# A two-block transformer kernel on one core: a reordered latent stage, and matmul operands at other byte offsets

## The chip, the core and the metric

The kernel runs on one core of a Trainium2 chip. A core has a matrix engine (TensorE, PE in the profile), three engines for elementwise work (VectorE or DVE, ScalarE or ACT, GpSimd or POOL), and SyncE (SP), which issues most of the loads. Each engine runs its own program in order; they meet through semaphores. Matmul operands lie in SBUF, 128 partitions wide; results go to eight PSUM banks. The metric is the device time of one execution in microseconds.

## The reference, cut to what matters

Two blocks over a sequence of 512 tokens and a width of 1,024, all in float32:

```python
# first block: layer 0 is a short convolution mixer, layer 1 latent attention
h = h + short_conv_mixer(rms_norm(h, ...), a_w_in, a_conv, a_w_out)
h = h + conv_ffn(rms_norm(h, ...), up 0, conv, down 0)
ckv = rms_norm(h, kv_in_norm) @ w_dkv                    # 1024 -> 256 + 64
c_kv, k_rope = ckv[..., :256], apply_rope(ckv[..., 256:], cos, sin)
kv = rms_norm(c_kv, kv_norm) @ w_ukv                     # 256 -> 8 heads x (128 + 128)
q = rms_norm(rms_norm(h, ...) @ w_dq, q_norm) @ w_uq     # 1024 -> 512 -> 8 x (128 + 64)
h = h + causal_attention(q, k, v) @ w_o
h = h + conv_ffn(rms_norm(h, ...), up 1, conv, down 1)
# second block: modulation from c, three mixers side by side
#   (spatial gating, stick breaking, dilated windows), then
x = x + (1 + gate1) * (mixers @ w_out)
x = x + (1 + gate2) * conv_ffn(..., up 2, conv, down 2); return rms_norm(x)
```

## The kernel before, in words

Activations lie transposed: features on the partitions, in chunks of 128, and the 512 tokens along the row. A product of one weight tile (8 blocks of 128 x 128) with an activation goes into one PSUM bank of 512 columns. To keep float32 accuracy both sides are split into a high half (fp32r) and a low half, and `dot` (lines 1466 to 1468) issues three matmuls for each block: high x high, high weights x low activation, low weights x high activation. `wide` runs `dot` over the eight chunks of an activation.

The high and low halves of activations have their own buffers: XH and XL (inputs of most products, all up stages among them), MH and ML (mixer output, stage A_OUT), HH and HL (hidden layer, the three down stages), QXH and QXL (input of DQ), CLH and CLL (k and v latent, input of UKV), OH and OL (attention output, stage WO). All of these, and the weight buffers WH and WL, begin at a multiple of LINE = 2,048 bytes. The buffers of one stage share memory with those of others by stacks that are closed again, and what is allocated after a pair in its stack begins behind it.

A weight tile comes by a DMA of SyncE into one of four raw slots. ScalarE copies it to WH (line 554, called by `hi`; `ahead(t)` waits until TensorE has done tile t and then converts tile t + 2), and GpSimd subtracts, WL = raw - WH (line 505). In the up stages VectorE makes WL instead (line 968). WH and WL have two slots each.

The stage that the change reorders lies between the first feed-forward network and the attention, about 550 to 625 us. TensorE's order: three products DKV (two chunks of the k and v latent, and the 64 k_rope features, doubled), four products DQ, then UKV in four tiles, then UQ. Between them it forms column sums of squares: N_KV inside the first DKV product, N_LK (norm of the k and v latent) after the second DQ product (line 1506), N_LQ (norm of the q latent) after the second product of UKV's first tile, by eight one-column matmuls (`token_squares`, line 1511).

VectorE's order: reciprocal rb; the eight low halves QXL (line 898); for each of two DKV products the eviction times rb into CL (line 1107) and the add of its square (line 887); the whole `rope` of the third DKV product (line 1081 eviction times rb into RA, 1086 four products of 32 partitions with the sine table, 1090 the product with the cosine table, 1097 the sum into KR); `inverse(N_LK)` (line 891, and a memset of acc, 893); CL times rbl (line 1113), CLL (898); then for each of four DQ products the eviction into QL (1118) and the add of its square; then the evictions of UKV.

ScalarE's order: squares of CL; `ahead(T0["DQ"])`; the root of N_LK (line 583); `ahead(T0["DQ"] + 1)`; CLH (line 710); then for k = 0 to 3 the square of QL's chunk k, with `ahead(T0["DQ"] + k)` in front of it for k = 2 and 3. `ahead(T0["DQ"] + 2)` is what converts the first tile of UKV.

Of the kernel before, what the change touches and what calls it, by code (L numbers as in the profile page):

```python
# [18 lines left out]
F32R = mybir.dt.float32r  # L19
# [15 lines left out]
KQ, KKV = Q_LORA // P, KV_LORA // P
# [20 lines left out]
LINE = 4 * S  # L56
# [61 lines left out]
def build(nc, w_tiles, ada_tiles, c_in, x_in, vec_in, const_in, rope_in, mask1_in, mask2_in, gsgu_in, wsp_in, pos_in, out):  # L118
    T0, M0, DONE_T, DONE_M = schedule()
# [5 lines left out]
    with ctx:  # L125
        def sb(name, shape, dt=F32, stack=ctx, align=32):
            return stack.enter_context(nc.sbuf_tensor(name, shape, dt, align_bytes=align))

        def sem(name):
            return ctx.enter_context(nc.semaphore(name))  # L130

# [18 lines left out]
        cos_t, sin_t = trig[:, 0, :], trig[:, 1, :]  # L150
        rb = sb("rb", [P, S])
        rbl = sb("rbl", [P, S])
        acc = sb("acc", [P, S])
# [3 lines left out]
        RA, RB = RAB[:, 0, :], RAB[:, 1, :]  # L157


        st = ExitStack()  # L160
        CV = sb("CV", [P, KD, S], F32, st)
        MH = sb("MH", [P, KD, S], F32R, st, align=LINE)
        ML = sb("ML", [P, KD, S], F32R, st, align=LINE)
        st.close()
        st = ExitStack()
        HH = sb("HH", [P, FF, S], F32R, st, align=LINE)
        HL = sb("HL", [P, FF, S], F32R, st, align=LINE)
        st2 = ExitStack()
        TG = sb("TG", [P, S + 16], F32, st2)
        TU = sb("TU", [P, S + 16], F32, st2)  # L170
# [6 lines left out]
        ADA_SLOT = (ada01[:, 0, :], ada01[:, 1, :], trig[:, :, :].rearrange("p a b -> p (a b)"))  # L177
        crow = RAB[:, :, :].rearrange("p a b -> p (a b)")
        st = ExitStack()
        QXH = sb("QXH", [P, KD, S], F32R, st, align=LINE)  # L180
        QXL = sb("QXL", [P, KD, S], F32R, st, align=LINE)
        st.close()
        st = ExitStack()
        KN = sb("KN", [P, HEADS, S], F32, st)
        VT = sb("VT", [P, HEADS, S], F32, st)
        KR = sb("KR", [P, S], F32, st)
# [6 lines left out]
        CLL = sb("CLL", [P, KKV, S], F32R, st2, align=LINE)  # L193
        QL = sb("QL", [P, KQ, S], F32, st2)
        st2.close()
        OH = sb("OH", [P, HEADS, S], F32R, st, align=LINE)
        OL = sb("OL", [P, HEADS, S], F32R, st, align=LINE)
        st.close()
        st = ExitStack()
        FT = sb("FT", [P, 12, S], F32, st)  # L200
# [37 lines left out]
        ps = [ctx.enter_context(nc.psum_tensor(f"ps{i}", [P, S], F32)) for i in range(8)]  # L238
# [4 lines left out]
        s_in = {n: sem(f"s_in_{n}") for n in ("x0", "x1", "x2", "x3", "c", "vec", "const", "rope", "gsgu", "wsp", "mask", "pos")}  # L243
# [5 lines left out]
        s_ev = sem("s_ev")  # L249
# [10 lines left out]
        s_ssum = sem("s_ssum")  # L260
        s_root = sem("s_root")
        s_rb = sem("s_rb")
# [21 lines left out]
        s_qk = sem("s_qk")  # L284
# [44 lines left out]
        def vcol(name, i):  # L329

            first = V[name][0]
            return vec[:, first + i:first + i + 1] if isinstance(i, int) else vec[:, bass.ds(i + first, 1)]
# [17 lines left out]
        N_A, N_F0, N_KV, N_LK, N_LQ, N_F1, N_FIN, N_F2, N_END = range(9)  # L350
# [3 lines left out]
        E_A, E_F0, E_KV, E_Q, E_F1, E_M2, E_F2 = range(7)  # L354

        XL0 = [KD * e for e in range(E_M2 + 1)] + [KD * E_M2 + KD // 2]
        RB_AT = {n: i for i, n in enumerate((N_A, N_F0, N_KV, N_LK, N_F1))}
# [184 lines left out]
        def _(act):  # L542
            ch = Chain(act, s_act)
# [136 lines left out]
            def a_b(i):  # L680
                for k in range(4):
                    ahead(T0["A_B"] + k, i, 4)
                    act.wait_ge(s_y, i * 4 + (k + 1))
                    apart()
                    nc.scalar.activation(at(MH, i * 4 + k), CU[:, :], ACT.Copy).then_inc(s_yh, 1)
            repeat(act, 2, a_b)
# [21 lines left out]
            for m in range(KKV):  # L708
                act.wait_ge(s_nb, NB_KV + m + 1)
                nc.scalar.activation(CLH[:, m, :], CL[:, m, :], ACT.Copy, scale=vcol("kv_norm", m)).then_inc(s_lh, 1)  # L710
            for k in range(KQ):
                if k > 1:
                    ahead(T0["DQ"] + k)
                act.wait_ge(s_ev, M0["DQ"] + k + 1)
                square(N_LQ, k, k, QL[:, k, :])
# [20 lines left out]
            for a in range(BLOCKS_A):  # L736
                L = (block_a(a)[1] + 1) * P
                if a >= 4:
# [7 lines left out]
                                     scale=stat[:, 3, a:a + 1]).then_inc(s_pn, 1)  # L746
# [127 lines left out]
        def _(dve):  # L874
            ch = Chain(dve, s_dve)
            v = nc.vector
# [6 lines left out]
            def add_square(n, m, k):  # L883
                dve.wait_ge(s_sq, m + (SQ0[n] + 1))
                if not (n == 0 and isinstance(m, int) and m == 0):
                    dve.wait_ge(s_acc, m + ACC0[n])
                v.tensor_tensor(acc[:, :], acc[:, :], SQ[:, k % 2, :], ALU.add).then_inc(s_acc, 1)  # L887

            def inverse(n, dst):
                dve.wait_ge(s_root, n + 1)  # L890
                v.reciprocal(dst[:, :], dst[:, :]).then_inc(s_rb, 1)
                dve.wait_ge(s_rb, RB_AT[n] + 1)
                ch.link(v.memset(acc[:, :], 0.0))
# [175 lines left out]

            ropes = [0]  # L1070

            def rope(M, dst, scale=1.0, by=None):


                if ropes[0]:
                    dve.wait_ge(s_qk, ropes[0])
                ropes[0] += 1
                product(M)
                x = ps[M % 4]
                if by is not None:  # L1080
                    v.tensor_tensor(RA[:, :], x[:, :], by[:, :], ALU.mult).then_inc(s_ev, 1)
                    dve.wait_ge(s_ev, M + 1)
                    x = RA
                for row in range(0, P, 32):
                    other = row ^ 32
                    ch.step(v.scalar_tensor_tensor(RB[row:row + 32, :], x[other:other + 32, :], scale,  # L1086
                                                   sin_t[other:other + 32, :], ALU.mult, ALU.mult))
                if by is not None:
                    ch.wait()
                ins = v.scalar_tensor_tensor(RA[:, :], x[:, :], scale, cos_t[:, :], ALU.mult, ALU.mult)  # L1090
                if by is None:
                    ins.then_inc(s_ev, 1)
                    dve.wait_ge(s_ev, M + 1)
                    ch.wait()
                else:
                    ch.link(ins)
                v.tensor_tensor(dst, RA[:, :], RB[:, :], ALU.add).then_inc(s_qk, 1)

            def take(aux, dst):
# [5 lines left out]
            for k in range(KKV):  # L1105
                product(M0["DKV"] + k)
                v.tensor_tensor(CL[:, k, :], ps[(M0["DKV"] + k) % 4][:, :], rb[:, :], ALU.mult).then_inc(s_ev, 1)
                add_square(N_LK, k, k)
            dve.wait_ge(s_in["rope"], 32)
            rope(M0["DKV"] + KKV, KR[:, :], by=rb)  # L1110
            inverse(N_LK, rbl)
            for m in range(KKV):
                v.tensor_tensor(CL[:, m, :], CL[:, m, :], rbl[:, :], ALU.mult).then_inc(s_nb, 1)
            for m in range(KKV):
                lo_half(CLH[:, m, :], CLL[:, m, :], CL[:, m, :], vcol("kv_norm", m), (s_lh, m + 1), s_ll)
            for k in range(KQ):
                product(M0["DQ"] + k)
                v.tensor_tensor(QL[:, k, :], ps[(M0["DQ"] + k) % 4][:, :], rb[:, :], ALU.mult).then_inc(s_ev, 1)
                add_square(N_LQ, k, k)

            for t in range(HEADS // 2):
                for j in range(4):
                    M = M0["UKV"] + 4 * t + j
# [20 lines left out]
            for h in range(HEADS):  # L1144
                M = M0["UQ"] + HEADS // 2 + h
# [303 lines left out]
        def _(pe):  # L1449
# [20 lines left out]
            def wide(t, M, i=0, per=0, before=None, src=(XH, XL), ready=True, within=None):  # L1470

                if ready:
                    tile_ready(t, i, per)
                bank_free(M, i, per)
                for k in range(KD):
                    if before:
                        before(k)
                    last = dot(ps[M % 4][:, :], t, k, src[0][:, k, :], src[1][:, k, :], k == 0, k == KD - 1)
                    if within is not None and k == 5:
                        sum_squares(within)  # L1480
                last.then_inc(s_pe, 1)
# [15 lines left out]
            def inputs(e):  # L1497

                if e < E_M2:
                    return lambda k: pe.wait_ge(s_xl, KD * e + k + 1)  # L1500
                return lambda k: pe.wait_ge(s_xlp, XLP0[e] + k // 2 + 1) if k % 2 else \
                    pe.wait_ge(s_xl, XL0[e] + k // 2 + 1)

            def sum_squares(n):
                pe.wait_ge(s_acc, ACC0[n + 1])
                mm(ps[4][:, :], cc("ones"), acc[:, :], start=True, stop=True).then_inc(s_ssum, 1)
# [37 lines left out]

            out_product("A_OUT", (MH, ML), lambda k: pe.wait_ge(s_yl, k + 1))

# [83 lines left out]
            for k in range(3):  # L1630
                wide(T0["DKV"] + k, M0["DKV"] + k, before=inputs(E_KV) if k == 0 else None,
                     within=N_KV if k == 0 else None)
            for k in range(KQ):
                wide(T0["DQ"] + k, M0["DQ"] + k, before=inputs(E_Q) if k == 0 else None, src=(QXH, QXL))
                if k == 1:
                    sum_squares(N_LK)
            for t in range(HEADS // 2):
                tile_ready(T0["UKV"] + t)
                for j in range(4):
                    M = M0["UKV"] + 4 * t + j  # L1640
# [16 lines left out]
            for t in range(6):  # L1657
                tile_ready(T0["UQ"] + t)
                for j in range(2):
                    M = M0["UQ"] + 2 * t + j  # L1660
# [12 lines left out]
            for a in range(BLOCKS_A + 4):  # L1673
                if a < BLOCKS_A and a % 2 == 0:
                    for c in (a, a + 1):
                        h, qb = block_a(c)
# [7 lines left out]
                    for c in (a, a + 1):  # L1684
                        h, qb = block_a(c)
# [13 lines left out]
                if 0 <= b:  # L1699
                    h, qb = block_a(b)  # L1700
# [304 lines left out]
```

## Time and profile before

| | |
|---|---|
| median of 3 runs | 1811.03 us (1807.66 to 1811.35) |
| profiled execution, its own time | 1807.92 us |
| its span in the profile | 1806.2 us |
| TensorE matmul busy | 97% of the span |
| VectorE busy | 64% |
| ScalarE busy | 38% |
| GpSimd busy | 22% |

Times in the trace count from the start of the span. A TensorE matmul's record is longer than the distance to the next one's start, because matmuls overlap; the pace of the engine is read from the distances of the starts. "Idle before" is the time in which the engine had nothing running ahead of an instruction, and behind the arrow stands what released it. The granted clock is 1.00 at 2.4 GHz and 0.50 at 1.2 GHz.

### The profile page before, as it was taken

The numbers are of one execution on the slowest core, as the hardware profiler recorded it, in microseconds if no ns is written. First come the engines' busy times: TensorE is split into PE (matmuls) and PEld (weight loads), VectorE is DVE, ScalarE is ACT, GpSimd is POOL, SyncE is SP. The second block draws the span as 40 slices with busy tenths as digits, with TensorE's granted clock in tenths as the row PEclk, the third lists the DMA queues.
The fourth block names the chain that finished last, engine by engine and source line by source line (L and its number), as shares of the span: only waits on it lengthen the run. The fifth ranks groups of instructions, "written<-read, shape, count | busy, mean of one in ns | idle before, by whom it ended". The sixth has DMA issues, their size and how long they took to land.

```text
span 1806.2 us, 22183 instructions
## 1 busy us (share of the span) xinstructions
PE 1749.3 (97%) x7818; PEld 1412.7 (78%) x7818; DVE 1150.2 (64%) x1498; ACT 694.5 (38%) x967; POOL 396.2 (22%) x170
## 2 busy tenths in 40 slices
PE   7999999999999899999999999999999899999997
PEld 6888788888887666778888888787558788888886
DVE  6566777776667765577777766574756577777222
ACT  4123444443223235444444322332563444444221
POOL 3444100001444330210000144444101300000343
PEclk9999999999999899999999999999999899999999
DMA  4332232224663220132322466322100232222331
GB/s 181 101 108 93 93 104 94 93 98 159 221 210 105 70 71 1 59 105 93 101 96 93 148 234 212 108 94 90 39 1 24 70 105 93 99 99 93 105 105 70
DMA packets 52187, 186.84 MB, mean 103 GB/s; under 512 B 5792, under 2 KB 6048, under 8 KB 52000
## 3 DMA queue, kind: packets, MB, share of 16 engines
q1 hardware_dynamic: 50832, 182.47, 29.8%
q10 hardware_dynamic: 1296, 3.58, 0.6%
q8 instruction: 37, 0.61, 0.1%
q14 instruction: 22, 0.18, 0.0%
HBM read 183.94 MB, written 2.10 MB: 103 GB/s over the span
## 4 chain that ended last, share of the span: by engine, by line
PE 87%; DVE 8%; ACT 2%; issue 1%; DMA 1%; POOL 0%; ACTq 0%; DVEq 0%; SPq 0%
PE ps L1466 26%; PE ps L1468 26%; PE ps L1467 26%; DVE RAB L1086 1%; PE ps L1680 1%; PE ps L1779 1%; PE ps L1746 1%; DMA X<-x_in 1%; PE ps L1687 1%; DVE stat L1165 1%; PE ps L1767 1%; PE ps L1706 0%; DVE QXL L898 0%; PE ps L1769 0%; DVE RAB L1090 0%
## 5 line engine op out<-in xcount | busy, mean ns | idle before, releaser
L505 POOL TENSOR_TENSOR WL<-raw,WH 128x1024 fp32r<-128x1024 f32 x157 | 385.1, 2453 | 1362.2 <-ACT WH L554 1362.2
L1466 PE MATMUL ps<-XH,WH 128*128 128x512 f32 x1496 | 587.6, 393 | 15.0 <-DVE XL L898 9.6
L1467 PE MATMUL ps<-XL,WH 128*128 128x512 f32 x1496 | 583.7, 390 | 0.0
L1468 PE MATMUL ps<-XH,WL 128*128 128x512 f32 x1496 | 583.6, 390 | 0.0
L554 ACT ACTIVATE WH<-raw 128x1024 fp32r<-128x1024 f32 x291 | 308.3, 1059 | 579.8 <-PE ps L1468 545.7
L1466 PEld LDWEIGHTS ps<-XH,WH 128*128 128x128 f32 x1496 | 281.9, 188 | 78.2 <-POOL WL L505 9.8
L1468 PEld LDWEIGHTS ps<-XH,WL 128*128 128x128 f32 x1496 | 281.8, 188 | 59.3
L1467 PEld LDWEIGHTS ps<-XL,WH 128*128 128x128 f32 x1496 | 281.9, 188 | 58.7 <-issue 1.0
L1467 PE MATMUL ps<-HL,WH 128*128 128x512 f32 x528 | 205.4, 389 | 0.0
L1466 PE MATMUL ps<-HH,WH 128*128 128x512 f32 x528 | 205.4, 389 | 0.0
L1468 PE MATMUL ps<-HH,WL 128*128 128x512 f32 x528 | 205.4, 389 | 0.0
L968 DVE TENSOR_TENSOR WL<-raw,WH 128x1024 fp32r<-128x1024 f32 x134 | 163.9, 1223 | 34.3 <-ACT WH L554 34.3
L628 ACT ACTIVATE HH<-CU 128x512 f32 (+1 forms) x66 | 41.8, 633 | 207.8 <-DVE CU L1010 135.6
L1467 PEld LDWEIGHTS ps<-HL,WH 128*128 128x128 f32 x528 | 99.1, 188 | 20.7
L1468 PEld LDWEIGHTS ps<-HH,WL 128*128 128x128 f32 x528 | 99.1, 188 | 20.7
L1466 PEld LDWEIGHTS ps<-HH,WH 128*128 128x128 f32 x528 | 99.1, 188 | 20.4
L887 DVE TENSOR_TENSOR acc<-acc,SQ 128x512 f32<-128x512 f32 x59 | 81.0, 1373 | 24.0 <-ACT SQ L603 18.6
L898 DVE SCALAR_TENSOR_TENSOR XL<-X,vec,XH (+1 forms) x32 | 57.0, 1796 | 36.7 <-ACT XH L601 27.6
L939 DVE TENSOR_TENSOR X<-ps,X 128x512 f32 (+1 forms) x32 | 22.1, 692 | 82.8 <-PE ps L1468 82.8
L943 DVE SCALAR_TENSOR_TENSOR X<-ps,gm,X 128x512 f32<-128x512 f32 x16 | 12.0, 751 | 98.3 <-PE ps L1468 98.3
L980 DVE TENSOR_TENSOR TU<-ps,rb 128x512 f32<-128x512 f32 x44 | 30.4, 692 | 59.1 <-PE ps L1468 59.1
L639 ACT ACTIVATE CG<-CG 128x512 f32<-128x512 f32 x44 | 27.8, 632 | 99.3 <-DVE CG L990 99.3
(262 smaller groups left out, 1995.7 us busy)
## 6 DMA issues: line engine op xcount, KB each, us to landing
raw<-w_tiles SPq DMA_DIRECT2D x291, 512.0 KB, 3.2
ada<-ada_tiles SPq DMA_DIRECT2D x32, 512.0 KB, 5.3
trig<-ada_tiles SPq DMA_DIRECT2D x16, 512.0 KB, 6.7
out_x<-X SPq DMA_DIRECT2D x8, 256.0 KB, 2.0
X<-x_in SPq DMA_DIRECT2D x2, 512.0 KB, 8.5
X<-x_in ACTq DMA_DIRECT2D x2, 512.0 KB, 8.2
RAB<-c_in SPq DMA_DIRECT2D x2, 512.0 KB, 4.6
MK<-mask_in ACTq DMA_DIRECT2D x1, 1024.0 KB, 5.2
```

What stands on the lines that cost most here:

```text
L505: nc.gpsimd.tensor_tensor(WL[k % SPL][:, :], raw[:, k, :], f32(WH[k % SPL][:, :]), ALU.subtract).then_inc(s_lo, 1)
L554: nc.scalar.activation(WH[t % SPL][:, :], raw[:, slot, :], ACT.Copy).then_inc(s_hi, 1)
L628: nc.scalar.activation(at(HH, jj), CU[:, :], ACT.Copy).then_inc(s_hh, 1)
L639: nc.scalar.activation(CG[:, :], CG[:, :], ACT.Silu, bias=vcol("conv_b", jj) if bias else 0.0)\
L887: v.tensor_tensor(acc[:, :], acc[:, :], SQ[:, k % 2, :], ALU.add).then_inc(s_acc, 1)
L898: v.scalar_tensor_tensor(dst_l, src, g, f32(dst_h), ALU.mult, ALU.subtract).then_inc(sem_l, 1)
L939: ins = v.tensor_tensor(at(X, m), bank, at(X, m), ALU.add)
L968: v.tensor_tensor(WL[t % SPL][:, :], raw[:, t % RAW, :], f32(WH[t % SPL][:, :]), ALU.subtract).then_inc(s_lov, 1)
L980: ins = v.tensor_tensor(pad[:, 2:S + 2], ps[M % 4][:, :], rb[:, :], ALU.mult)
L1466: mm(bank, h, xh, start=first, stop=False)
L1467: mm(bank, h, xl, start=False, stop=False)
L1468: return mm(bank, lo, xh, start=False, stop=last)
```

## The change

In the latent stage: TensorE forms the sum N_LK inside the second DQ product (after its sixth chunk) instead of after it. VectorE evicts both CL chunks, then adds both squares, evicts k_rope times rb into RA, and goes to the reciprocal rbl at once (the memset of acc comes before the reciprocal). The rotation of k_rope is cut up: two of its four sine products come after the evictions of DQ 0 and 1, two after DQ 2, the cosine product (now a plain product of two tiles) after DQ 3, and the sum into KR after the last add of a square. ScalarE calls `ahead(T0["DQ"] + 2)`, UKV's first tile, before all squares of QL, and `ahead(T0["DQ"] + 3)` ahead of the last.

In the memory: a new helper allocates a pair of activation buffers in one room that begins at a multiple of 2,048 bytes, and leaves 32 bytes free ahead of MH and ML, 16 ahead of HH and HL, 256 ahead of QXH and QXL and 1,040 ahead of OH and OL. XH, XL, CLH, CLL, WH and WL stay at multiples of 2,048.

```diff
+        def two_at(name, chunks, remainder, stack):
+            first = remainder // 4
+            room = stack.enter_context(nc.sbuf_tensor(name, [P, first + 2 * chunks * S], F32R, align_bytes=LINE))
+            return [room[:, first + h * chunks * S:first + (h + 1) * chunks * S].rearrange("p (c s) -> p c s", s=S)
+                    for h in range(2)]
...
-        MH = sb("MH", [P, KD, S], F32R, st, align=LINE)
-        ML = sb("ML", [P, KD, S], F32R, st, align=LINE)
+        MH, ML = two_at("MHL", KD, 32, st)
...
-        HH = sb("HH", [P, FF, S], F32R, st, align=LINE)
-        HL = sb("HL", [P, FF, S], F32R, st, align=LINE)
+        HH, HL = two_at("HHL", FF, 16, st)
...
+        QXH, QXL = two_at("QXHL", KD, 256, st)
...
+        OH, OL = two_at("OHL", HEADS, 1040, st)
...
+            ahead(T0["DQ"] + 2)
             for k in range(KQ):
-                if k > 1:
+                if k == KQ - 1:
                     ahead(T0["DQ"] + k)
...
+            def rotate(row, x, scale):
+                other = row ^ 32
+                ch.step(v.scalar_tensor_tensor(RB[row:row + 32, :], x[other:other + 32, :], scale,
+                                               sin_t[other:other + 32, :], ALU.mult, ALU.mult))
...
+            for k in range(KKV):
                 add_square(N_LK, k, k)
-            dve.wait_ge(s_in["rope"], 32)
-            rope(M0["DKV"] + KKV, KR[:, :], by=rb)
-            inverse(N_LK, rbl)
+            product(M0["DKV"] + KKV)
+            v.tensor_tensor(RA[:, :], ps[(M0["DKV"] + KKV) % 4][:, :], rb[:, :], ALU.mult).then_inc(s_ev, 1)
+            dve.wait_ge(s_ssum, N_LK + 1)
+            ch.link(v.memset(acc[:, :], 0.0))
+            dve.wait_ge(s_root, N_LK + 1)
+            v.reciprocal(rbl[:, :], rbl[:, :]).then_inc(s_rb, 1)
+            dve.wait_ge(s_rb, RB_AT[N_LK] + 1)
...
-            for k in range(KQ):
+            def latent(k):
                 product(M0["DQ"] + k)
                 v.tensor_tensor(QL[:, k, :], ps[(M0["DQ"] + k) % 4][:, :], rb[:, :], ALU.mult).then_inc(s_ev, 1)
-                add_square(N_LQ, k, k)
+            latent(0)
+            latent(1)
+            dve.wait_ge(s_in["rope"], 32)
+            dve.wait_ge(s_ev, M0["DKV"] + KKV + 1)
+            rotate(0, RA, 1.0)
+            rotate(32, RA, 1.0)
+            add_square(N_LQ, 0, 0)
+            latent(2)
+            add_square(N_LQ, 1, 1)
+            rotate(64, RA, 1.0)
+            rotate(96, RA, 1.0)
+            add_square(N_LQ, 2, 2)
+            latent(3)
+            ch.wait()
+            ch.link(v.tensor_tensor(RA[:, :], RA[:, :], cos_t[:, :], ALU.mult))
+            add_square(N_LQ, 3, 3)
+            v.tensor_tensor(KR[:, :], RA[:, :], RB[:, :], ALU.add).then_inc(s_qk, 1)
+            ropes[0] += 1
...
-                wide(T0["DQ"] + k, M0["DQ"] + k, before=inputs(E_Q) if k == 0 else None, src=(QXH, QXL))
-                if k == 1:
-                    sum_squares(N_LK)
+                wide(T0["DQ"] + k, M0["DQ"] + k, before=inputs(E_Q) if k == 0 else None, src=(QXH, QXL),
+                     within=N_LK if k == 1 else None)
```

## Rows read from the trace of the kernel before

**Rows 1.** The page: TensorE's busy share, and its clock in 40 slices.
```profile
PE 1749.3 (97%) x7818; PEld 1412.7 (78%) x7818; DVE 1150.2 (64%) x1498; ACT 694.5 (38%) x967; POOL 396.2 (22%) x170
...
PEclk9999999999999899999999999999999899999999
```
**Rows 2.** TensorE's waits: who was waited for, total us, times, longest.
```profile
PE ps L1466 <- POOL WL L505: 8.1, 1, 8.1
```
**Rows 3.** TensorE's timeline, 578 to 605 us: start, us, instruction, count.
```profile
578.98 1.02 PE L1506 MATMUL ps<-acc,cst 128*128 128x512 f32 x2
...
590.54 0.39 PE L1468 MATMUL ps<-QXH,WL 128*128 128x512 f32 x1
599.00 0.79 PE L1466 MATMUL ps<-CLH,WH 128*128 128x512 f32 x1 [8.07 <-POOL WL L505]
599.60 0.63 PE L1467 MATMUL ps<-CLL,WH 128*128 128x512 f32 x1
600.02 0.63 PE L1468 MATMUL ps<-CLH,WL 128*128 128x512 f32 x1
...
604.17 0.95 PE L1511 MATMUL ps<-cst,acc 128*128 128x1 f32 x8
```
**Rows 4.** Stretches: us, then busy us by engine, granted clock, DMA share, GB/s.
```profile
594.00:598.00 4.00, 0.00 (x0) 0.00 (x0) 2.61 (x5) 2.64 (x4) 1.40 (x1) 0.50 0.00 0
600.00:604.00 4.00, 4.00 (x11) 3.10 (x10) 2.19 (x3) 0.63 (x1) 1.74 (x1) 0.50 0.69 214
...
1283.40:1286.70 3.30, 3.09 (x10) 2.54 (x11) 1.24 (x4) 1.63 (x6) 0.00 (x0) 0.50 0.24 94
```
**Rows 5.** TensorE's timeline in the first down stage.
```profile
480.06 0.39 PE L1466 MATMUL ps<-HH,WH 128*128 128x512 f32 x1
...
483.46 0.39 PE L1466 MATMUL ps<-HH,WH 128*128 128x512 f32 x1
```
**Rows 6.** VectorE's timeline in the latent stage.
```profile
572.50 0.68 DVE L1107 TENSOR_TENSOR CL<-ps,rb 128x512 f32<-128x512 f32 x1
...
577.20 4.74 DVE L1086 SCALAR_TENSOR_TENSOR RAB<-RAB,trig 32x512 f32<-32x512 f32 x4
581.98 2.77 DVE L1090 SCALAR_TENSOR_TENSOR RAB<-RAB,trig 128x512 f32<-128x512 f32 x1
...
585.39 3.34 DVE L891 RECIPROCAL rbl<-rbl 128x512 f32<-128x512 f32 x1
```
**Rows 7.** Lines 887 and 1086, 570 to 603 us: ns min/median/max.
```profile
L887 DVE TENSOR_TENSOR acc<-acc,SQ x6: 691/692/1902, 573.9 to 600.8; 128x512 f32<-128x512 f32 x6
...
L1086 DVE SCALAR_TENSOR_TENSOR RAB<-RAB,trig x4: 681/685/2597, 577.2 to 581.3; 32x512 f32<-32x512 f32 x4
```
**Rows 8.** ScalarE's timeline in the latent stage.
```profile
580.04 0.69 ACT L583 ACTIVATE rbl<-ps,epsc 128x512 f32<-128x512 f32 x1 [3.25 <-PE ps L1506]
...
595.49 1.04 ACT L554 ACTIVATE WH<-raw 128x1024 fp32r<-128x1024 f32 x1
```
**Rows 9.** GpSimd's timeline in the latent stage.
```profile
576.87 2.39 POOL L505 TENSOR_TENSOR WL<-raw,WH 128x1024 fp32r<-128x1024 f32 x1 [6.16 <-ACT WH L554]
581.75 2.44 POOL L505 TENSOR_TENSOR WL<-raw,WH 128x1024 fp32r<-128x1024 f32 x1 [2.50 <-ACT WH L554]
```
**Rows 10.** Matmul groups by shape: busy us, mean ns, idle before.
```profile
L1466 PE MATMUL ps<-HH,WH 128*128 128x512 f32 x528 | 205.4, 389 | 0.0
...
L1466 PE MATMUL ps<-MH,WH 128*128 128x512 f32 x64 | 24.9, 389 | 0.0
...
L1466 PE MATMUL ps<-QXH,WH 128*128 128x512 f32 x32 | 13.0, 406 | 0.8 <-DVE QXL L898 0.8
```
**Rows 11.** TensorE's timeline in the stick-breaking stage.
```profile
1303.34 0.81 PE L1769 MATMUL ps<-SP,cst 128*128 128x384 f32 x2
1303.98 0.38 PE L1770 MATMUL ps<-SP,cst 128*128 128x128 f32 x2
```
**Rows 12.** A stretch of the first up stage, columns as in rows 4.
```profile
200.00:430.00 230.00, 229.99 (x1015) 190.09 (x1015) 167.68 (x214) 98.90 (x130) 0.00 (x0) 1.00 0.30 98
```

More of the change, by code:

```diff
@@ L179, in build @@
         st = ExitStack()
-        QXH = sb("QXH", [P, KD, S], F32R, st, align=LINE)
-        QXL = sb("QXL", [P, KD, S], F32R, st, align=LINE)
+        QXH, QXL = two_at("QXHL", KD, 256, st)
         st.close()
@@ L195, in build @@
         st2.close()
-        OH = sb("OH", [P, HEADS, S], F32R, st, align=LINE)
-        OL = sb("OL", [P, HEADS, S], F32R, st, align=LINE)
+        OH, OL = two_at("OHL", HEADS, 1040, st)
         st.close()
@@ L1070, in _, with rope @@
             ropes = [0]
-            def rope(M, dst, scale=1.0, by=None):
-                if ropes[0]:
-                    dve.wait_ge(s_qk, ropes[0])
+            def rotate(row, x, scale):
+                other = row ^ 32
+                ch.step(v.scalar_tensor_tensor(RB[row:row + 32, :], x[other:other + 32, :], scale,
+                                               sin_t[other:other + 32, :], ALU.mult, ALU.mult))
+            def rope(M, dst, scale=1.0):
+                dve.wait_ge(s_qk, ropes[0])
                 ropes[0] += 1
@@ L1079, in rope @@
                 x = ps[M % 4]
[L1080 to L1083, printed above, removed]
                 for row in range(0, P, 32):
[L1085 to L1096, printed above, removed]
+                    rotate(row, x, scale)
+                v.scalar_tensor_tensor(RA[:, :], x[:, :], scale, cos_t[:, :], ALU.mult, ALU.mult).then_inc(s_ev, 1)
+                dve.wait_ge(s_ev, M + 1)
+                ch.wait()
                 v.tensor_tensor(dst, RA[:, :], RB[:, :], ALU.add).then_inc(s_qk, 1)
@@ L1115, in _ @@
                 lo_half(CLH[:, m, :], CLL[:, m, :], CL[:, m, :], vcol("kv_norm", m), (s_lh, m + 1), s_ll)
-            for k in range(KQ):
+            def latent(k):
                 product(M0["DQ"] + k)
                 v.tensor_tensor(QL[:, k, :], ps[(M0["DQ"] + k) % 4][:, :], rb[:, :], ALU.mult).then_inc(s_ev, 1)
-                add_square(N_LQ, k, k)
+            latent(0)
[11 more added lines that the diff above has]
+            latent(3)
+            ch.wait()
+            ch.link(v.tensor_tensor(RA[:, :], RA[:, :], cos_t[:, :], ALU.mult))
+            add_square(N_LQ, 3, 3)
+            v.tensor_tensor(KR[:, :], RA[:, :], RB[:, :], ALU.add).then_inc(s_qk, 1)
+            ropes[0] += 1
             for t in range(HEADS // 2):
```

## The prediction

> **What bounds the kernel now.** I read the page first, then TensorE's waits, TensorE's own timeline, the timelines of VectorE, ScalarE and GpSimd around the longest stall that the change can touch, and last the matmul groups. The page says that TensorE is busy for 97% of 1806.2 us at full clock in nearly every slice [rows 1]: what shortens this kernel either removes a hole in TensorE's stream or makes each matmul cheaper. The change tries both, in different places.
>
> The hole: the list of waits has one of 8.1 us, for a weight low half (WL) from GpSimd [rows 2]. It is the start of the UKV products: the last DQ matmul starts at 590.54 and the next at 599.00 [rows 3]. After that the reader is to see two spacings: at 599.60 and 600.02 starts are 0.427 us apart, and the granted clock of the stretches around them is 0.50 [rows 4], so the hole costs a second time, in slow matmuls. Twelve of them run before the column sums of the q norm (token squares) start at 604.17 [rows 3]. That start is my yardstick, since everything behind it in UKV follows the same order before and after.
>
> The stream: in a down stage 15 matmuls take 483.46 - 480.06 = 3.40 us, 226.7 ns each [rows 5]. At 2.4 GHz 512 columns alone are 213.3 ns, and at the lower level the spacing is 426.7 ns, exactly 512 columns at 1.2 GHz [rows 3, 4]. So at full clock each matmul pays 13.3 ns beyond its columns, with equal remainders everywhere. Whatever those 13.3 ns are, they are the room for the second half of the change.
>
> **Why the hole is there.** VectorE runs in program order. It takes CL0 at 572.50, and then does the whole rotation of the key (the four products at 577.20 take 4.74 us, the cosine product at 581.98 takes 2.77) before the reciprocal at 585.39 and all that hangs on it [rows 6]. The first DQ tile is evicted only after CLL, about 592.2, so ScalarE, which had to see two DQ squares before it turned to UKV's first weights, converts them at 595.49 [rows 8], GpSimd's low half follows, and TensorE starts. Two of VectorE's times are swollen: an add takes 691 ns undisturbed and 1902 at worst, a rotation 681 and 2597 [rows 7]. The long rotation at 577.20 begins 0.33 us after a GpSimd subtraction (576.87, 2.39 us) and ends 0.57 after that ends; the cosine product at 581.98 is likewise caught by the one at 581.75 [rows 6, 9]. Two-input operations from SBUF and GpSimd's subtractions exclude each other here; that sets the new order's price.
>
> **The latent stage step by step.** Estimates in us of the same trace.
> - CL0 and CL1 evicted back to back save nothing, since DQ0 is still being multiplied. The two adds end near 575.3, the k_rope product (RA) is out at 575.9. TensorE now forms the k norm's sum inside DQ1 after 18 of its 24 matmuls: six matmuls, 1.36 us, earlier than its 578.98 [rows 3], so 577.6, done 578.65. The root, 580.04 before [rows 8], comes at 578.7 and ends at 579.4. The sum's time on TensorE (about 0.9) stays, only its place moves.
> - The memset (0.48) lies under the root. The reciprocal takes its 3.34 [rows 6], 579.4 to 582.75, where it was 585.39 to 588.73: 6.0 earlier, because the rotation is no longer ahead of it.
> - The CL products (0.69 each) meet GpSimd's subtraction for DQ3, now about 581.2 to 583.6, and end at 585.0; CLH and CLL follow to 586.5. UKV0's weights now wait on DQ2 alone (585.5) and on CLH: converted 585.7 to 586.75, subtracted 586.85 to 589.25. TensorE comes free at 590.8. The 8.1 us wait is gone, and so is the first slow stretch.
> - What is late next: the q norm's sum, which TensorE wants after UKV's second product, 590.8 + 12 x 0.2267 = 593.6. VectorE: DQ0, DQ1 evicted 586.5 to 587.8; the first rotation is held by the subtraction of UKV0 until 589.8; second rotation 590.5, add 591.2, DQ2 591.8, add 592.5, two rotations 593.9. ScalarE squares DQ2 to 592.5, converts UKV1's weights to 593.5, and GpSimd subtracts 593.6 to 596.0. The third add is caught (596.6), DQ3 evicted 597.25, its square 597.95, with the cosine product (now one tensor_tensor, 0.69) under it, last add 598.7. Token squares at 598.8.
> - Queued behind the waits that were added: behind the wait for the root stand CL, CLL and all DQ evictions, none of which TensorE wants before 590.8. Banks: DQ3 needs the k_rope bank (free 575.9), UKV's third product needs DQ2's (591.8, wanted after 598.8). KR is added after the last add; the key copies wait for it, but the next bank TensorE needs is 2.7 us of matmuls away. No DMA is issued or moved; four weight loads stay ahead.
>
> Start of the token squares: 604.17 - 598.8 = 5.4 us earlier. Off that goes the clock. TensorE is idle for some 5.0 us (593.6 to 598.8) instead of 8.07. Before, it ran at half rate for 5.1 us after it resumed, 599.00 to about 604.1; a hole of 2.94 us ahead of 1282.6 was also followed by 0.50 [rows 4]. With the same 5.1 us, 1.0 of it the token squares, the rest costs (5.1 - 1.0)/2 = 2.1. Net 5.4 - 2.1 = 3.3 us. Bounds: 7.4 if the third add escapes GpSimd's subtraction (1.9 more) and the clock never falls (2.1 more); 1 if the slow stretch lasts 3 us longer and costs 1.5 more and one more eviction is caught. I take 3.3. Nothing later gives it back: from there to the end each stage waits for TensorE or for what the stage itself makes.
>
> **The offsets.** Matmuls concerned: MH/ML 3 x 64 = 192, HH/HL 3 x 528 = 1584, QXH/QXL 3 x 32 = 96 and OH/OL as many as MH/ML, 192 [rows 10]: 2064 in all. The 4,488 on XH/XL are as before. Of these 2064, the DQ ones are partly off the path (DQ ends 1.5 us after UKV0's weights are ready); that is under 1 us. What the trace has on unequal remainders: within a tile the weight block moves by 512 bytes from product to product while the spacing stays 226.7, so differences of multiples of 512 cost nothing. Nothing shows 16, 32, 256 or 1,040 at this pace. The nearest is plain fp32: SP against the constants, which by the sizes allocated ahead of them begin at byte 2,432 (384 beyond 2,048), steps two 384-column passes in 1303.98 - 1303.34 = 0.64 us [rows 11], which is 2 x 768 cycles at 2.4 GHz, no loss. That is two cycles a column, where reads have twice the room. By the nearest rows each matmul then gains at most 13.3 ns (2064 x 13.3 = 27.5 us) and, taking the same loss once more as the other end, loses 27.5; the far end, every matmul at the fp32 pace of 426.7 ns, would be 413 us, and nothing speaks for it. I take zero: it is what the 512-byte steps and rows 11 show. New addresses of VectorE's and ScalarE's operands I cost at nothing: in 230 us of the first up stage VectorE is busy for 167.68 and ScalarE for 98.90 while TensorE never pauses [rows 12], so they have slack; if that cover were gone, 1% more on VectorE would be 1.7 us there.
>
> One rule is weighed here. The row: 226.7 ns at full clock [rows 5]. The Trainium skill, "TensorE: Matmul & The Clock Gate", section "Back-to-back issue gap", gives 512/2.4 + 2.5 = 215.8 ns for an isolated matmul, so the trace disagrees by 10.9 ns, and if the offsets brought that back the sum would have another 2064 x 10.9 = 22 us less. "SBUF — State Buffer", section "Who interferes with whom", says that TensorE reads moving operand and weights through independent ports and never waits on anyone; by that the offsets do nothing and the sum stands at 3.3. The equal spacing at 512-byte steps agrees with this one, but cannot say why 13.3 ns are lost.
>
> **The rivals.**
> - Slower: moving rows and weights that are read together disturb each other unless their remainders agree modulo 512 (which is all that the trace covers). Place: mainly the three down stages; price p per matmul. It eats the gain from p = 1.6 ns (3.3/2064), and the kernel is over 0.2% slower from p = 3.4 ns. With half the present loss more (6.7 ns) 1811.0 - 3.3 + 13.8 = 1821.5; with all of it 1835. For: 13.3 ns are lost in each matmul only at full clock, when both reads are closest. Against: rows 11, and no dependence on the block.
> - Faster: equal remainders are themselves the collision, and an offset of 16 bytes (HH, and OH at 1,040) undoes it: 1776 x 13.3 = 23.6, so 1784; if only some offsets work or half the loss goes, 1790 to 1802. For: the same 13.3 ns. Against: the same spacing for four block positions.
> - The latent stage gives more: GpSimd's subtraction misses the third add, TensorE waits 3 us, the clock costs 1.5: 5.9, so 1805. A matter of 0.5 us in order.
> - The change does not do what it says, the wait just moves behind the token squares: under 1 us, 1810.5.
>
> **How the numbers follow.** The profiled execution took 1807.92, span 1806.2; its sum is 1804.6. It lies 3.1 under the median of 1811.03, whose runs reach from 1807.66 to 1811.35, so the forecast on the median is 1811.03 - 3.3 = 1807.7. Chances: no effect of offsets 0.58 (latent as forecast 0.37, more 0.15, moved wait 0.06), slower offsets 0.21, faster offsets 0.21. Own range of the likeliest, 1803 to 1811. For 8 in 10 I reach to 1789 and 1822: outside are the deep ends of both offset cases, some 0.08 each. About 0.2% (3.6 us) is what a measurement tells here. Faster: 0.21 + 0.15 + a third of 0.37 and a bit of the slow end, 0.47. Same: the rest of the likeliest, the moved wait and the mildest offset losses, 0.35. Slower: 0.18.
>
> **What would show it.** Steps: TensorE has no wait for WL at UKV's start, but one of 4 to 5.5 us before the token squares, with clock 0.50 after it; the reciprocal on rbl starts near 579.4, ahead of any rotation; one add in the DQ part is over 1.5 us long. Offsets: the spacing of HH matmuls stays 226.7 ns, and the down stages last what they did. The prediction is wrong if that spacing differs by over 1.6 ns, or if the wait before the token squares is gone or over 7 us.

## The result, and the profile after

The changed kernel takes 1816.14 us (median of 13 runs, 1814.27 to 1821.43) against 1808.68 for the kernel before, of which there are now 13 runs too (1807.66 to 1814.2). The ratio is 1.0043 (95% interval 1.0036 to 1.005): slower by some 7.8 us, where I had forecast 3.3 less. (The forecast of 1807.7 stood on a median of 3 runs, 1811.03, which lies 2.4 us above the median of 13.) The profiled executions differ by 1813.0 - 1806.2 = 6.8 us of span.

First TensorE's waits in the changed kernel. The wait of 8.1 us for WL [rows 2] is gone, and one of 4.9 us for an add stands in its place (total us, times, longest):

```profile
PE ps L1531 <- DVE acc L891: 4.9, 1, 4.9
```

TensorE's timeline of the changed kernel in the latent stage, to be laid beside [rows 3]:

```profile
557.71 1.13 PE L1526 MATMUL ps<-acc,cst 128*128 128x512 f32 x2 [0.68 <-DVE acc L891]
...
597.23 0.39 PE L1488 MATMUL ps<-CLH,WL 128*128 128x512 f32 x1
602.50 1.86 PE L1531 MATMUL ps<-cst,acc 128*128 128x1 f32 x8 [4.89 <-DVE acc L891]
604.23 0.77 PE L1486 MATMUL ps<-CLH,WH 128*128 128x512 f32 x1
604.80 0.63 PE L1487 MATMUL ps<-CLL,WH 128*128 128x512 f32 x1
605.23 0.63 PE L1488 MATMUL ps<-CLH,WL 128*128 128x512 f32 x1
...
609.92 0.62 PE L1487 MATMUL ps<-CLL,WH 128*128 128x512 f32 x1
...
628.13 0.47 PE L1486 MATMUL ps<-XH,WH 128*128 128x512 f32 x1 [0.78 <-issue]
```

and two more starts of the kernel before, for the distances:

```profile
553.70 1.13 PE L1506 MATMUL ps<-acc,cst 128*128 128x512 f32 x2 [0.70 <-DVE acc L887]
...
625.98 0.47 PE L1466 MATMUL ps<-XH,WH 128*128 128x512 f32 x1 [0.78 <-issue]
```

The reader is to see three things. The stage begins 4.01 us late, which the offset buffers used ahead of it will explain: the N_KV sum starts at 557.71, before at 553.70. Measured from there, the token squares come after 604.17 - 553.70 = 50.47 us before and 602.50 - 557.71 = 44.79 us after, 5.7 us earlier. And after them the spacing is 0.427 us until about 610.3, so part of the gain is lost again in half-rate matmuls: UQ starts 70.42 us after the N_KV sum, where before it was 72.28. The stage gained 1.9 us.

VectorE's timeline of the changed kernel shows the steps of the forecast:

```profile
579.28 0.68 DVE L1107 TENSOR_TENSOR RAB<-ps,rb 128x512 f32<-128x512 f32 x1
582.78 0.48 DVE L1109 MEMSET acc<- 128x512 f32 x1 [2.82 <-PE ps L1526]
583.44 3.35 DVE L1111 RECIPROCAL rbl<-rbl 128x512 f32<-128x512 f32 x1 [0.17 <-ACT rbl L586]
...
597.69 2.72 DVE L891 TENSOR_TENSOR acc<-acc,SQ 128x512 f32<-128x512 f32 x1
600.33 0.68 DVE L1120 TENSOR_TENSOR QL<-ps,rb 128x512 f32<-128x512 f32 x1
...
601.76 0.69 DVE L891 TENSOR_TENSOR acc<-acc,SQ 128x512 f32<-128x512 f32 x1 [0.15 <-DVE RAB L1136]
```

and GpSimd's shows what holds the add of 2.72 us:

```profile
597.32 2.54 POOL L508 TENSOR_TENSOR WL<-raw,WH 128x1024 fp32r<-128x1024 f32 x1 [4.27 <-ACT WH L557]
```

The loss is in the down, A_OUT and WO stages. TensorE's starts, 30 matmuls apart, in A_OUT (MHL), the first down stage (HHL) and WO (OHL) of the changed kernel:

```profile
160.00 0.39 PE L1488 MATMUL ps<-MHL,WL 128*128 128x512 f32 x1
167.00 0.39 PE L1488 MATMUL ps<-MHL,WL 128*128 128x512 f32 x1
...
480.02 0.39 PE L1487 MATMUL ps<-HHL,WH 128*128 128x512 f32 x1
486.97 0.40 PE L1487 MATMUL ps<-HHL,WH 128*128 128x512 f32 x1
...
745.14 0.39 PE L1487 MATMUL ps<-OHL,WH 128*128 128x512 f32 x1
752.09 0.40 PE L1487 MATMUL ps<-OHL,WH 128*128 128x512 f32 x1
```

7.00/30 = 233.3 ns for MH/ML (32 bytes off), 6.95/30 = 231.7 for HH/HL (16) and OH/OL (1,040), where all were at 226.7 [rows 5]. The QX group kept its mean of 406 ns, as in [rows 10], at 256 bytes off. So 192 x 6.6 + 1584 x 5.0 + 192 x 5.0 ns = 1.3 + 7.9 + 1.0 = 10.2 us more. (A_OUT and the first down stage, 1.3 and a third of 7.9, are nearly all of the late start of 4.01 us.) With the latent stage, 10.2 - 1.9 = 8.3, which is 1.5 more than the 6.8 of the two spans. That much is clock: at 1355 to 1358 us the trace of before has a half-rate stretch that the trace of after has not. Counted by position in TensorE's order, the same matmul starts 4.7 us later in the changed kernel ahead of this stretch (1351.70 and 1356.44) and 3.2 us later behind it (1380.23 and 1383.44). The other shifts between the two traces are about 1 us at most and nearly cancel. The two stretches, of the kernel before and of the changed one (columns as in rows 4, the granted clock is 0.95 and 1.00):

```profile
1340.00:1376.00 36.00, 33.41 (x173) 25.18 (x171) 26.02 (x55) 18.46 (x30) 0.00 (x0) 0.95 0.00 1
```

```profile
1345.00:1380.00 35.00, 32.41 (x176) 24.37 (x177) 26.61 (x56) 18.60 (x28) 0.00 (x0) 1.00 0.00 1
```

### The profile page after: what moved, and what is told of

It is laid out like the page before. It is cut to its first block, busy times and chain, and to the rows that moved or that the text cites. A ratio compares the mean times of both kernels' runs of the same rounds, so it can differ in the third digit from the quotient of the medians.

```text
span 1813.0 us, 22244 instructions
## 1 busy us (share of the span) xinstructions
PE 1759.5 (97%) x7818; PEld 1412.9 (78%) x7818; DVE 1148.2 (63%) x1498; ACT 694.2 (38%) x967; POOL 394.9 (22%) x170
## 4 chain that ended last, share of the span: by engine, by line
PE 87%; DVE 8%; ACT 2%; issue 2%; DMA 1%; POOL 0%; DVEq 0%; ACTq 0%; SPq 0%
PE ps L1486 26%; PE ps L1487 26%; PE ps L1488 26%; DVE RAB L1079 1%; PE ps L1699 1%; PE ps L1798 1%; PE ps L1765 1%; DMA X<-x_in 1%; PE ps L1706 1%; DVE stat L1185 1%; DVE acc L891 1%; PE ps L1725 0%; PE ps L1786 0%; PE ps L1621 0%; PE ps L1805 0%
## 5 line engine op out<-in xcount | busy, mean ns | idle before, releaser
L1487 PE MATMUL ps<-HHL,WH 128*128 128x512 f32 x528 | 208.1, 394 | 0.0
L1488 PE MATMUL ps<-HHL,WL 128*128 128x512 f32 x528 | 208.1, 394 | 0.0
L1486 PE MATMUL ps<-HHL,WH 128*128 128x512 f32 x528 | 208.1, 394 | 0.0
L631 ACT ACTIVATE HHL<-CU 128x512 f32 (+1 forms) x66 | 41.7, 632 | 208.7 <-DVE CU L1014 136.2
L1487 PEld LDWEIGHTS ps<-HHL,WH 128*128 128x128 f32 x528 | 99.3, 188 | 23.1
L1488 PEld LDWEIGHTS ps<-HHL,WL 128*128 128x128 f32 x528 | 99.3, 188 | 23.0
L1486 PEld LDWEIGHTS ps<-HHL,WH 128*128 128x128 f32 x528 | 99.3, 188 | 23.0
```

What stands on the lines that cost most here:

```text
L631: nc.scalar.activation(at(HH, jj), CU[:, :], ACT.Copy).then_inc(s_hh, 1)
L1486: mm(bank, h, xh, start=first, stop=False)
L1487: mm(bank, h, xl, start=False, stop=False)
L1488: return mm(bank, lo, xh, start=False, stop=last)
```

## The experiments

**One part at a time.** The latent order alone, with the four `two_at` lines turned back into aligned pairs; and the offsets alone, in the old order:

```diff
-        MH, ML = two_at("MHL", KD, 32, st)          # e1_latent; HH/HL, QXH/QXL, OH/OL alike
+        MH = sb("MH", [P, KD, S], F32R, st, align=LINE)
+        ML = sb("ML", [P, KD, S], F32R, st, align=LINE)
...
-        HH = sb("HH", [P, FF, S], F32R, st, align=LINE)     # e2_offsets, on the kernel before
-        HL = sb("HL", [P, FF, S], F32R, st, align=LINE)
+        HH, HL = at_remainders("HHL", FF, (16, 16), st)     # MH/ML (32, 32), OH/OL (1040, 1040)
```

> The reordered latent stage alone, all operand buffers at multiples of 2,048 bytes as before. Theory (two independent parts): the token squares of the q norm start about 5.7 us earlier than before and some 3 to 4 us of that are lost to half-rate matmuls behind the 4.9 us wait, so 1.9 us less than before (1 to 4), ratio 0.998 to 0.9995, and every fp32r spacing at full clock is 226.7 ns. Rival (the reorder itself is what costs): over 3 us slower than before.

> The offsets alone, old order of the latent stage: MH/ML at 32, HH/HL at 16, OH/OL at 1,040 bytes beyond a multiple of 2,048; QXH/QXL left at 0, since the old order would write over them, and 256 bytes cost nothing in the changed kernel's spacing. Theory: 192 matmuls x 6.6 ns + 1584 x 5.0 + 192 x 5.0 = 1.3 + 7.9 + 1.0 = 10.2 us slower than before, ratio 1.0055. Rival (the spacing is made up elsewhere, or the time came from the latent stage): under 5 us slower.

Measured: the latent order alone 1805.17 us, ratio 0.9984 (0.9973 to 0.9995), 2.9 us less; the offsets alone 1818.66, ratio 1.005 (1.0035 to 1.0065), 9 us more, or 10.3 by the medians (1808.39 for the kernel before in this series). The first timeline is of the latent order alone, with no offsets, and shows the same 4.89 us wait (its first row is the start of the N_KV sum, its last the start of UQ); the second, of the offsets alone, has the changed kernel's spacing, (487.14 - 480.19)/30 = 231.7 ns:

```profile
553.83 1.12 PE L1532 MATMUL ps<-acc,cst 128*128 128x512 f32 x2 [0.68 <-DVE acc L897]
...
598.62 1.65 PE L1537 MATMUL ps<-cst,acc 128*128 128x1 f32 x7 [4.89 <-DVE acc L897]
...
605.19 0.40 PE L1494 MATMUL ps<-CLH,WL 128*128 128x512 f32 x1
...
623.62 0.47 PE L1492 MATMUL ps<-XH,WH 128*128 128x512 f32 x1 [0.78 <-issue]
```

```profile
480.19 0.40 PE L1474 MATMUL ps<-HHL,WL 128*128 128x512 f32 x1
487.14 0.39 PE L1474 MATMUL ps<-HHL,WL 128*128 128x512 f32 x1
```

In the latent order alone the token squares come 44.79 us after the N_KV sum, as in the changed kernel, but the half-rate spacing ends at 605.19, 6.6 us after the wait and not 7.8, and UQ starts 69.79 us after the sum: the stage gained 2.5 us there. The two parts have opposite signs, and their sum, 9.0 - 2.9 = 6.1 us, agrees with the 7.8 of the changed kernel within the intervals; the loss is the offsets'.

**Whose remainder?** In the next kernel WH and WL were moved by 32 bytes, and with them what is allocated behind (HH/HL come to 32 by that; QXH/QXL were put to 32 and OH/OL to 64, MH/ML back to 0):

```diff
-        WH = [sb(f"WH{i}", [P, TILE], F32R, align=LINE) for i in range(SPL)]
-        WL = [sb(f"WL{i}", [P, TILE], F32R, align=LINE) for i in range(SPL)]
+        WROOM = sb("WHL", [P, 8 + 2 * SPL * TILE], F32R, align=LINE)
+        WH = [WROOM[:, 8 + i * TILE:8 + (i + 1) * TILE] for i in range(SPL)]
+        WL = [WROOM[:, 8 + (SPL + i) * TILE:8 + (SPL + i + 1) * TILE] for i in range(SPL)]
```

> The weight buffers WH and WL are at 32 bytes beyond a multiple of 2,048; XH/XL, MH/ML, CLH/CLL at 0, HH/HL and QXH/QXL at 32, OH/OL at 64. Theory R (the difference between the moving operand's and the weights' remainders decides): HH and QXH step 226.7 ns, OH 233.3 (difference 32), XH and MH slower than 226.7 (difference -32). Rival M (the moving operand's own remainder decides): XH and MH 226.7, HH and QXH 233.3, OH as MH at 64 in the run before. Rival W (the weights' own remainder decides too): all stages slower than 226.7.

```profile
300.26 0.40 PE L1493 MATMUL ps<-XH,WHL 128*128 128x512 f32 x1
307.26 0.40 PE L1493 MATMUL ps<-XH,WHL 128*128 128x512 f32 x1
...
480.40 0.39 PE L1493 MATMUL ps<-HH,WHL 128*128 128x512 f32 x1
487.20 0.39 PE L1493 MATMUL ps<-HH,WHL 128*128 128x512 f32 x1
```

XH, untouched at a multiple of 2,048, is now at 233.3 ns, and HH, at 32 like the weights, at 226.7. MH (difference -32) and OH (+32) are at 233.3 too. It is the difference that counts: theory R, and both rivals fall. The time, one run, was 1835.09 us: the 4,488 matmuls on XH/XL, at 6.6 ns each, pay 29.6 us. In the same trace UKV runs for a while at the lower clock, with a difference of -32:

```profile
612.44 0.63 PE L1492 MATMUL ps<-CLL,WHL 128*128 128x512 f32 x1
612.87 0.63 PE L1493 MATMUL ps<-CLH,WHL 128*128 128x512 f32 x1
613.29 0.63 PE L1491 MATMUL ps<-CLH,WHL 128*128 128x512 f32 x1
```

There the spacing is 0.427 us as with equal remainders [rows 3]. At half rate no price is seen for this difference; the others have no half-rate rows.

**Which differences?** Three kernels in the new order, other numbers in the four pairs.

> New order, other remainders: MH/ML 64, HH/HL 48, QXH/QXL 128, OH/OL 96 beyond a multiple of 2,048. Theory A (a modulus of 64 bytes in the moving address): 64 and 128 step 226.7 ns, 48 as 16 (231.7) or 32 (233.3), 96 as 32 (233.3). Theory B (modulus 256): none of the four is at 226.7. Theory C (a matter of near distances only): 16 and 32 are slow because they are small; 64 and more all step 226.7.

> New order; differences to the weights' remainder: MH/ML 192, HH/HL 240, QXH/QXL 80, OH/OL 8. Theory P (period 256 in the difference, symmetric): 240 as 16, 556 cycles of 2.4 GHz; 192 as 64, 550; 80 at 560; 8 between 544 and 556. Rival (period 256, not symmetric, one side may even be below 544): 240 differs from 556 by over 4 cycles.

> New order; MH/ML 112, HH/HL 64, QXH/QXL 512, OH/OL 256. Theory P (period 256): OH 544 cycles, QXH as in the kernel before (546), HH 550 as MH had at 64, MH 560. Rival (256 was hidden in QXH by other waits): OH above 550.

Mean spacing over each stage at full clock, from the starts in the traces, and cycles of 2.4 GHz:

| difference, bytes | pair | ns | cycles |
|---|---|---|---|
| 0 | all | 226.7 | 544 |
| 8 | OH/OL | 232.7 | 558 |
| 16; 1,040 | HH/HL; OH/OL | 231.7 | 556 |
| 32 | MH/ML (OH/OL in two other kernels: 233.3) | 233.3 | 560 |
| 48 | HH/HL | 233.3 | 560 |
| 64 | HH/HL (MH/ML 229.1) | 229.7 | 551 |
| 96 | OH/OL | 233.4 | 560 |
| 112 | MH/ML | 231.1 | 555 |
| 128 | QXH/QXL | 233.0 | 559 |
| 192; 240 | MH/ML; HH/HL | 233.3 | 560 |
| 256 | OH/OL | 226.9 | 544 |

(80 in QXH/QXL gave 231.2; 512 gave 227.5 where the aligned buffers have 227.6 to 228.0 in that short stage.) Most differences were tried in one pair of buffers only; those tried in two, 32, 64 and 16 with 1,040, agree within 0.7 ns. Of the first run's theories A and C are out, and B, a modulus of 256, is left, which the 256 in OH/OL confirms. My theory of a symmetric pattern failed: 192 is not as 64, nor 240 as 16; and 80 and 112, expected at 560 cycles, are at 555. Nothing tried is below 544 cycles: no offset tried beats the aligned layout.

**Each operand for itself?** High and low half at different remainders:

> High and low halves at different remainders, weights at 0: MH 0 and ML 16, HH 0 and HL 32, QXH 0 and QXL 96, OH 16 and OL 0. Of three matmuls of a block two move the high half and one the low half. Theory (each matmul pays for its own moving operand): mean spacing in MH/ML 226.7 + 5.0/3 = 228.4, HH/HL 226.7 + 6.6/3 = 228.9, OH/OL 226.7 + 2 x 5.0/3 = 230.0. Rival (what is paid is paid when the address steps between buffers or for the pair): the three means are equal to 226.7 or to the full 231.7 and 233.3.

> New order; high and low half at different remainders again: MH 0 and ML 256, HH 0 and HL 16, QXH and QXL 0, OH and OL 32, weights at 0. Theory (only the distance modulo 256 between what is read at the same time matters, and a low half 16 away disturbs the loads on both sides of it): MH/ML 544 cycles, HH/HL 552 to 557, OH/OL 560. Rival (the step from one operand's remainder to the other's costs by itself): MH/ML over 548.

With a high half at 0 and a low one at 32 (HH/HL) the mean was 231.7 ns, where "each pays for its own" gives 228.9; with 0 and 16 it was 232.0 (MH/ML) and again 232.0 (HH/HL of the second run, 557 cycles), no less than when both are at 16 (231.7); 16 and 0 (OH/OL) 231.1. So "each pays for its own" is wrong: at 16 one displaced matmul of three costs as much as three, and at 32 it costs 5.0 of the 6.6 ns. It isn't the step between buffers as such, since 0 and 256 run at the full pace:

```profile
160.03 0.39 PE L1491 MATMUL ps<-MHL,WL 128*128 128x512 f32 x1
166.83 0.39 PE L1491 MATMUL ps<-MHL,WL 128*128 128x512 f32 x1
```

(6.80/30 = 226.7). Nor is it only the displaced matmul or the one ahead of it: with 0 and 16 in HH/HL (weights at 0) the mean distance from high x high to the low half is 230.6 ns, from there to the high half 231.8, and from that to the next block, where both operands lie at 0, it is 233.6. Which reads meet stays open.

**Where the latent gain went.** Three orders, all aligned. First, the rotation moved out of the DQ part, one sine product behind each key copy of UKV's first tile, and ScalarE's `ahead(T0["DQ"] + 3)` behind the last square:

```diff
             add_square(N_LQ, 0, 0)
...
             add_square(N_LQ, 3, 3)
...
                         v.tensor_copy(KN[:, 4 * t + j, :], ps[M % 4][:, :]).then_inc(s_ev, 1)
+                        if t == 0:
+                            rotate(32 * j, RA, 1.0)
```

> Aligned buffers, and a latent stage in which the rotation is taken out of the DQ part altogether: its four sine products come between the evictions of UKV's first tile, and ScalarE converts UKV's second weight tile after the last DQ square. Theory (the last add is late only because rotations and a GpSimd subtraction stand ahead of it): TensorE reaches the token squares without a wait of over 0.5 us and the clock stays at 1.00, 9 to 10.6 us less than before, about 1799. Rival (VectorE has too much to do in this stage whatever the order, and the wait moves into UKV): a wait of 2 us or more elsewhere in UKV, 3 to 6 us less than before.

1804.88 us, 0.9981 (0.997 to 0.9991): no better than the latent order alone, the rival's number. The token squares start at once, at 593.88, as the theory had it, but then:

```profile
605.04 2.08 PE L1542 MATMUL ps<-cst,nt 128*128 128x128 f32 x8 [4.53 <-DVE nt L1070]
```

VectorE's timeline of that kernel says why; ScalarE has the root ready at 599.03, but the reciprocal of 0.18 us stands behind three products, one held by GpSimd for 2 us:

```profile
599.12 2.76 DVE L1084 SCALAR_TENSOR_TENSOR RAB<-RAB,trig 32x512 f32<-32x512 f32 x1
...
604.08 0.69 DVE L1153 TENSOR_TENSOR KR<-RAB 128x512 f32<-128x512 f32 x1
604.81 0.18 DVE L1070 RECIPROCAL nt<-nt 128x4 f32<-128x4 f32 x1
```

The half-rate stretch was not avoided either: the granted clock was 0.50 from 604.6 to 608.0. Second, root and reciprocal first:

```diff
-            ahead(T0["UKV"])
             token_root(N_LQ, Q_LORA)
+            ahead(T0["UKV"])
...
+                        if t == 0 and j == 0:
+                            token_inverse(N_LQ)
+                            ch.link(v.memset(acc[:, :], 0.0))
+                        if (t, j) in ((0, 1), (0, 3), (1, 0), (1, 2)):
+                            rotate(32 * (2 * t + j // 2), RA, 1.0)
...
+                if t == 3:
+                    ch.wait()
+                    ch.link(v.tensor_tensor(RA[:, :], RA[:, :], cos_t[:, :], ALU.mult))
+                    v.tensor_tensor(KR[:, :], RA[:, :], RB[:, :], ALU.add).then_inc(s_qk, 1)
```

> Aligned buffers; the q norm's root and reciprocal are taken as soon as the token squares are done (ScalarE ahead of UKV's third weight tile, VectorE after the first key copy), and the rotation is spread over UKV's first two tiles, its end at the last. Theory (the wait of 4.5 us in the run before is for a reciprocal of 0.2 us that stands behind the rotation, not for a VectorE that has too much to do): no TensorE wait over 1 us between 592 and 620, no half-rate stretch there, 6 to 10 us less than before, near 1800. Rival (too much work for VectorE in this stage): the wait shows up again at a bank or at UQ's input, 3 to 4 us less than before, as in the two runs before.

1802.02 us, 0.9959 (0.9945 to 0.9974). UQ starts at 615.83 instead of 625.98, 10.1 us earlier, and half of that is lost again in two waits of UQ for a rope (VectorE's rotation of a q product):

```profile
634.86 0.47 PE L1489 MATMUL ps<-XH,WH 128*128 128x512 f32 x1 [2.43 <-DVE RAB L1095]
...
640.17 0.50 PE L1489 MATMUL ps<-XH,WH 128*128 128x512 f32 x1 [2.34 <-DVE RAB L1095]
```

Both theories were half right: no wait between 592 and 615, but two behind. The cosine product and the sum (1.73 and 0.69 us, at 617.45) stood ahead of UQ's first rope, which starts 4.10 us after UQ (619.93 - 615.83). Third, the pieces put where VectorE only waits:

```diff
+            rotate(0, RA, 1.0)                      # in the wait for the k norm's sum
             dve.wait_ge(s_ssum, N_LK + 1)
...
                         if t == 0 and j == 0:
+                            rotate(32, RA, 1.0)     # in the wait for the q norm's root
                             token_inverse(N_LQ)
...
+                        if (t, j) in ((0, 1), (0, 3)):
+                            rotate(64 + 32 * (j // 2), RA, 1.0)
+                        # cosine product after (1, 0), sum into KR after (1, 2)
```

> Aligned buffers; as the early-root version, but the rotation is cut into the places where VectorE only waits: one sine product in the wait for the k norm's sum, one in the wait for the q norm's root, two among the key copies, cosine product and sum among UKV's second tile, none of it left for the end of UKV. Theory (what remained in that version were two waits of 2.4 us in UQ, for ropes that VectorE began 2.4 us late behind the rest of the rotation): those two waits fall under 1.5 us each, 8 to 11 us less than before, near 1799, ratio 0.994 to 0.9955. Rival (UQ is bound by VectorE's four ropes wherever the rotation stands): the same time as the early-root version within 1 us, ratio 0.9955 to 0.9965.

1799.7 us, 0.995 (0.9936 to 0.9963): 9 us less than the kernel before and, by the medians of two series, 16 less than the changed one; the lowest of the versions run, though its interval overlaps that of the second order. The longest wait of UQ for a rope is now 0.4 us. The first rope starts 3.12 us after UQ (619.54 - 616.42), so 1.0 us earlier than in the second order. That alone does not make up for two waits of 2.4 us; the rest is GpSimd. The last step of the first rope, in the second order and then in the third:

```profile
622.73 2.40 POOL L514 TENSOR_TENSOR WL<-raw,WH 128x1024 fp32r<-128x1024 f32 x1 [4.10 <-ACT WH L563]
623.53 2.14 DVE L1098 TENSOR_TENSOR QR<-RAB 128x512 f32<-128x512 f32 x1
```

```profile
623.14 0.69 DVE L1098 TENSOR_TENSOR QR<-RAB 128x512 f32<-128x512 f32 x1
623.33 2.76 POOL L514 TENSOR_TENSOR WL<-raw,WH 128x1024 fp32r<-128x1024 f32 x1 [4.55 <-ACT WH L563]
```

In the second order this step starts 0.8 us behind a subtraction and takes 2.14 us, and those of the next two ropes take 1.81 and 1.77; in the third order it starts 0.19 us ahead of the subtraction and takes 0.69, as the next two do. That is 3.6 us, and with the 1.0 it covers the two waits, 4.8. Neither expectation had this order in view: that part of the third order's gain is luck.

Stretches of the third order and, in the second fence, of the second (columns as in rows 4):

```profile
593.00:617.00 24.00, 22.76 (x108) 18.50 (x107) 23.39 (x31) 8.27 (x11) 10.82 (x5) 1.00 0.26 88
617.00:641.00 24.00, 23.60 (x104) 19.18 (x103) 20.45 (x30) 4.25 (x4) 9.94 (x5) 1.00 0.26 88
```

```profile
617.00:641.00 24.00, 19.23 (x83) 15.30 (x83) 23.19 (x28) 3.18 (x3) 8.79 (x4) 0.99 0.27 88
```

TensorE went from 19.23 to 23.60 busy of 24 us there, and VectorE from 23.19 to 20.45: 2.4 us of cosine product and sum went out of the stretch where VectorE sets the pace, and 3.6 us of being held by GpSimd went with them. (Other work of VectorE came into the window in their place.)

## Why the prediction was wrong, point by point

- **The steps of the latent stage were right.** Against the start of the N_KV sum, the token squares were forecast 5.4 us earlier and came 5.7 earlier; the wait ahead of them was forecast at 5.0 and is 4.89; the third add is the one caught by GpSimd's subtraction, 2.72 us instead of 0.69. The Trainium skill, "SBUF — State Buffer", section "Who interferes with whom", has this as a lock on a shared pair of ports; the trace agrees (2.72 us, ending 0.55 us after the subtraction of 2.54 us does).
- **The clock's term was too small.** I took 5.1 us at half rate, of which the token squares would lose nothing. In the changed kernel it was nearly 8 (602.50 to about 610.3), and the token squares themselves took 1.73 us to the next matmul instead of 0.81. So 5.7 became 1.9 instead of 3.3. In the kernel with the latent order alone the same wait was followed by 6.6 us at half rate, and the stage gained 2.5; by the ratio the whole kernel gained 2.9 us (0.9 to 4.9), so my 3.3 is compatible with it but not confirmed by it.
- **The step that failed: "I take zero" for the offsets.** It is 10.2 us by the spacings, and 9 us by the ratio of the kernel with the offsets alone. I had named the mechanism as a rival (moving rows and weights disturb each other unless their remainders agree modulo 512, p from 1.6 ns eats the gain) and given it 0.21. The modulus is 256, p is 5.0 to 6.6 ns, and the rival's 6.7 ns, on the median that was 2.4 us high, put 1821.5 beside the measured 1816.14.
- **Why I took zero.** Two readings carried it. The 512-byte steps of the weight block show only that multiples of 512 are free; I read them as if they spoke for smaller distances. And [rows 11], plain fp32 at two cycles a column, says nothing of one cycle a column: with twice the time for each, at the lower clock, a difference of -32 shows no loss either. What pointed the other way stood in the same text: 13.3 ns are lost in each matmul at full clock and none at half. (That these are reads that meet is still not shown.) A loss that appears only at the highest rate had to be bounded at that rate.
- **The rule.** The page of the Trainium skill just named says that TensorE's two read ports are independent and that TensorE never waits on anyone. Here the spacing of the same instructions goes from 226.7 to 233.3 ns and back with nothing but the distance between moving operand and weights. The measurement decides: for fp32r at full clock the time depends on both addresses together, so the two reads are not independent here.
- "No effect on VectorE's and ScalarE's operands" and the counts of matmuls held: the 10.2 us from TensorE's spacing lie inside the interval of the offsets alone (6.3 to 11.8 us).

## What to carry to other kernels

When a matmul's spacing is longer than its columns at full clock, ask what else is read in that time, and bound a change of addresses by rows at that same rate. In a stream of fp32r matmuls of 512 columns, put moving operands and weights at the same remainder of 256 bytes, low halves too. And when a chain is taken off one wait, write down what each engine has queued behind it: work that is only moved comes back where that engine sets the pace next, and the places to put it are the waits it already has. Where two engines exclude each other, look at which of their operations comes first: a shift of 1 us turned three sums of 0.69 us into some 2 us each.

## What the runs showed of the hardware that I had not expected

The spacing of 512-column fp32r matmuls at 2.4 GHz depends on the difference of the byte addresses of moving operand and weights modulo 256: 544 cycles at 0, 551 at 64 (550 in another pair), 555 to 560 at all other distances tried, 8 bytes included. At 1.2 GHz the one distance seen, -32, steps 0.427 us as equal remainders do. With two operands at different distances the mean is not the weighted mean (557 cycles with one of three matmuls 16 off, 556 with all three). Why 32 cycles remain at equal remainders stays open, as does the exception at 64. After the same wait of 4.89 us TensorE ran at half rate for 7.8 us in the changed kernel and for 6.6 in the latent order alone.
